# Block sums of streamed weights: made by transfers that add to their target, in place of GpSimd additions, in a two-block transformer kernel on one core

## The chip, the core and the metric

The kernel runs on one NeuronCore of one Trainium2 chip. The metric is the device time of one execution in microseconds (us). Five engines work side by side: TensorE (PE: matmuls, and PEld: its weight loads), VectorE (DVE), ScalarE (ACT), GpSimd (POOL) and SyncE (SP), which here only issues transfers. Data lies in SBUF (on chip, 128 partitions), in PSUM (eight banks of 128 x 512 words, where the matmuls accumulate) and in HBM, where the weights lie.

## The reference

Two transformer blocks are applied to one sequence of 512 tokens with width 1024, in 32-bit floats. What matters here is the last step of each block, a wide layer pair with 4096 hidden columns:

```
x = x + jnp.square(jax.nn.relu(h @ w_up[l])) @ w_down[l]
...
hid = jnp.square(jax.nn.relu(jnp.einsum('bsd,df->bsf', n2, w_up[l])))
mlp_out = jnp.einsum('bsf,fd->bsd', hid, w_down[l])
h = h + rms_norm_2(mlp_out, norm_mlp_post[l])
```

Before these steps come attention, a gated linear attention and cross attention in the first block, and a gated spatial layer and dilated attention in the second. The change does not touch them.

## The kernel before

**Precision.** Every 32-bit operand is split in two parts: a high part (made by ScalarE as a copy into a rounded type, `w_hi`, `a_hi`) and the rest (made by VectorE or GpSimd as a subtraction, `w_lo`, `a_lo`). Each product is three matmuls: high by high, low by high, high by low (lines 1236 to 1238).

**Weights.** They come as tiles of 128 x 1024 words (512 KB). SP issues their transfers in a fixed order, each behind a wait on `lo_w`, the count of the tiles that VectorE has split. Ordinary tiles land in two buffers `w_raw`; split tiles lie in eight slots of `w_hi` and `w_lo`. A tile is split when a slot is free, so VectorE's subtraction at line 1944 is what makes a `w_raw` buffer free for the next transfer.

**The wide layers.** The 4096 hidden columns are done in eight chunks of 512, in the order up(0), up(1), down(0), up(2), down(1), ... up(7), down(6), down(7). An `up` takes four tiles and gives `sq`, the squared hidden values (four PSUM banks, 96 matmuls). The first six `down` of each block are done with seven products of blocks instead of eight (a scheme of Strassen and Winograd): `block_sums` makes four sums s1 to s4 of blocks of `sq` on GpSimd, and the step `tsum` makes four sums t1 to t4 of the four weight tiles b11, b12, b21, b22. A product is 12 matmuls into two PSUM banks, (4, 5) for even products and (6, 7) for odd ones, and VectorE adds each bank to its target (line 2042, called draining the bank below). So product n+2 can start only when VectorE has drained the banks of product n. With the `up` this is 180 matmuls in a round of one `up` and one `down`; there are 12 rounds with seven products in the program.

**Order around the change.** Every engine walks through the same list of steps. In `up`, at its first step, ScalarE and VectorE split units 0 to 3 of the coming `down`, at its third step units 4 and 5, at its last step unit 6 (`tile_done` tells that a slot is free). During the products they split the four tiles of the next `up`, called raw 1 to raw 4 below, one after each of the products 0 to 3 (in half of the rounds inside the loop, after products 2 to 5). At a product, VectorE first drains the two banks and then splits what belongs to this step. The middle rounds are a hardware loop of two turns with two rounds each.

Of the kernel before, what the change touches and what calls it, by code (L numbers as in the profile page):

```python
# [31 lines left out]
ALU = mybir.AluOpType  # L32
# [84 lines left out]
UNITS = ("b11", "b21", "t2", "t1", "t3", "b22", "t4")  # L117
INTO = ("q1", (0, 0), "q6", "q5", "q7", (0, 1), (1, 0))
# [11 lines left out]
class Step:  # L130

    def __init__(self, kind, banks, fill, *, n=0, h=0, p=None, out=None, major=None, src=None, dst=None, rows=KC,
# [20 lines left out]
        self.nmax = nmax  # L154
        self.splits_lo = splits if splits_lo is None else splits_lo

class Schedule:
# [139 lines left out]
    def bank_steps(self, out, major, src, rows=KC, banks=4, halves=1, ready=None, blk=0, mid=None, dst=None, p=None,  # L298
# [77 lines left out]
    def products(self, dst, first=False):  # L376
# [68 lines left out]
def make_schedule():  # L445
# [103 lines left out]
    def run_mlp(dst, after_last, last):  # L549
# [172 lines left out]
    s.add("tsum", held=[s.n_down, 0], ready=all_out())  # L722
# [90 lines left out]
    s.add("tsum", held=[s.n_down, 0], ready=[])  # L813
# [45 lines left out]
def two_blocks(nc, a, out):  # L859

    s = make_schedule()
    with ExitStack() as ctx:
# [129 lines left out]
        t2 = place("t2", "mid", [WORDS], skip=28 * KB)  # L992
        t1 = place("t1", "more", [WORDS])
        t4 = place("t4", "more", [WORDS], skip=4 * KB)
        w_down = nc.alloc_sbuf_tensor_at("w_down", [P, 4, WORDS], F32, offset=base + region["const"] + phase)
        top_, low_ = slice(0, 2 * P), slice(2 * P, T)
        parts = (sq[:, 0:2, top_], sq[:, 2:4, top_], s2[:], s1[:], s3[:], s4[:], sq[:, 2:4, low_])
        part_sums = (0, 0, 3, 1, 2, 4, 0)
# [42 lines left out]
        down_in = [sem(f"down_in{n}") for n in range(4)]  # L1041
        sum_w = sem("sum_w")
# [44 lines left out]
        def landed(kind, raw):  # L1087
# [5 lines left out]
            if kind in ("t1", "t2", "t4"):  # L1093
                return {"t1": t1, "t2": t2, "t4": t4}[kind][:]
# [44 lines left out]
        def block_sums(eng, st, turn):  # L1139
# [3 lines left out]
            eng.tensor_tensor(s1[:], sq[:, 0:2, low_], sq[:, 2:4, low_], ALU.add).then_inc(sum_a, 1)  # L1143
            eng.wait_ge(sum_a, at(st.sum_a, turn, 1))
            eng.tensor_tensor(s3[:], sq[:, 0:2, top_], sq[:, 0:2, low_], ALU.subtract).then_inc(sum_a, 1)
            eng.tensor_tensor(s2[:], s1[:], sq[:, 0:2, top_], ALU.subtract).then_inc(sum_a, 1)
            eng.wait_ge(sum_a, at(st.sum_a, turn, 3))
            eng.tensor_tensor(s4[:], sq[:, 2:4, top_], s2[:], ALU.subtract).then_inc(sum_a, 1)

        def part_lo(eng, st, j, turn):  # L1150

            eng.wait_ge(hi_a, at(st.held, turn, j + 1))
            eng.tensor_tensor(a_lo[:, j], parts[j], a_hi[:, j], ALU.subtract).then_inc(lo_a, 1)

# [29 lines left out]
        def _(sp):  # L1184
# [7 lines left out]
            def load(kind, slot, tile, free, turn):  # L1192
                wait(sp, lo_w, at(free, turn))
                t = at(tile, turn)
                src = a["weights"][t] if isinstance(t, int) else a["weights"][bass.ds(t, 1)].rearrange("o p w -> p (o w)")
                if kind == "raw":
                    sp.dma_start(w_raw[:, slot, :], src).then_inc(raw_in[slot], 16)
                else:
                    sp.dma_start(w_down[:, slot, :], src).then_inc(down_in[slot], 16)
# [413 lines left out]
        def _(act):  # L1613
# [8 lines left out]
            def split(st, turn):  # L1622
                for n, slot, kind, raw, load, free in st.splits:
# [7 lines left out]
                    else:  # L1631
                        act.wait_ge(sum_w, at([4 * load[0], 4 * load[1]], turn, ("t1", "t2", "t3", "t4").index(kind) + 1))
# [298 lines left out]
        def _(dve):  # L1931
# [14 lines left out]
            def fold(st):  # L1946
# [5 lines left out]
                then(dve.tensor_tensor(q["q6"], q["q6"], q["q1"], ALU.add))  # L1952
                dve.tensor_tensor(x12, x12, q["q6"], ALU.add)
                then(dve.tensor_tensor(q["q7"], q["q7"], q["q6"], ALU.add))
                then(dve.tensor_tensor(x21, x21, q["q7"], ALU.add))
                if st.dst == "y":
                    dve.tensor_tensor(x22, q["q7"], q["q5"], ALU.add)
                else:
                    then(dve.tensor_tensor(q["q7"], q["q7"], q["q5"], ALU.add))
                    dve.tensor_tensor(x22, x22, q["q7"], ALU.add)  # L1960
# [649 lines left out]
```

## Time and profile before

| | |
|---|---|
| time, median of 3 runs (lowest to highest) | 1569.46 us (1569.41 to 1570.41) |
| span of the profiled execution | 1569.9 us |
| TensorE busy | 1553.6 us, 99% |
| VectorE busy | 989.6 us, 63% |
| ScalarE busy | 663.7 us, 42% |
| GpSimd busy | 483.5 us, 31% |
| moved by transfers | 164.34 MB, 105 GB/s over the span |
| granted TensorE clock in the windows read | 1.00 |

The profile names no other time for the profiled execution than its span. A row of a timeline gives the start, the duration, the engine, the line, the operation with target and sources, and in brackets how long the engine had been idle and on whom it waited. Where a row says x2, two operations were merged and the duration is that of both. The first wide layers lie at about 431 to 748 us, the second at about 1215 to 1561 us.

### The profile page before, as it was taken

The numbers are of one execution on the slowest core, as the hardware profiler recorded it, in microseconds if no ns is written. First come the engines' busy times: TensorE is split into PE (matmuls) and PEld (weight loads), VectorE is DVE, ScalarE is ACT, GpSimd is POOL, SyncE is SP. The second block draws the span as 40 slices with busy tenths as digits, with TensorE's granted clock in tenths as the row PEclk, the third lists the DMA queues.
The fourth block names the chain that finished last, engine by engine and source line by source line (L and its number), as shares of the span: only waits on it lengthen the run. The fifth ranks groups of instructions, "written<-read, shape, count | busy, mean of one in ns | idle before, by whom it ended". The sixth has DMA issues, their size and how long they took to land.

```text
span 1569.9 us, 21076 instructions
## 1 busy us (share of the span) xinstructions
PE 1553.6 (99%) x7772; PEld 1307.9 (83%) x7772; DVE 989.6 (63%) x1187; ACT 663.7 (42%) x1091; POOL 483.5 (31%) x283
## 2 busy tenths in 40 slices
PE   9999999999999999999999999999999999999998
PEld 7788888888888888888888898988888988888886
DVE  5453876335487777776664746347356677777766
ACT  5352565244354443443533334543334454434432
POOL 2442000000037776762310000020013047777732
PEclk9999999999999999999999999999999999999999
DMA  6422135321412232214232232343334322213133
GB/s 247 135 81 81 41 99 185 94 81 53 135 54 108 108 108 107 107 54 154 85 101 85 67 94 68 95 141 118 110 122 156 135 108 98 85 50 134 68 116 121
DMA packets 44997, 164.34 MB, mean 105 GB/s; under 512 B 5584, under 2 KB 5800, under 8 KB 44272
## 3 DMA queue, kind: packets, MB, share of 16 engines
q1 hardware_dynamic: 40608, 144.82, 28.4%
q0 software_dynamic: 4304, 18.36, 3.4%
q8 instruction: 56, 0.92, 0.2%
q14 instruction: 29, 0.24, 0.0%
HBM read 158.88 MB, written 5.85 MB: 105 GB/s over the span
## 4 chain that ended last, share of the span: by engine, by line
PE 94%; DVE 4%; ACT 1%; DMA 1%; issue 1%; POOL 0%; DVEq 0%; ACTq 0%; SPq 0%; POOLq 0%
PE banks L1236 29%; PE banks L1238 29%; PE banks L1237 29%; PE banks L1535 1%; PE banks L1414 1%; DVE nmax L2228 1%; DVE w_lo L1944 1%; DMA w_raw<-in_weights 1%; PE banks L1380 1%; PE banks L1353 0%; PE banks L1597 0%; DVE banks L2227 0%; PE banks L1573 0%; PE banks L1565 0%; PE banks L1524 0%
## 5 line engine op out<-in xcount | busy, mean ns | idle before, releaser
L1236 PE MATMUL banks<-act_hi,w_hi 128*128 128x512 f32 (+1 forms) x1088 | 413.3, 380 | 3.1 <-DVE act_lo L2110 3.1
L1944 DVE TENSOR_TENSOR w_lo<-w_raw,w_hi 128x1024 fp32r<-128x1024 f32 x216 | 280.4, 1304 | 208.4 <-ACT w_hi L1633 204.4
L1238 PE MATMUL banks<-act_hi,w_lo 128*128 128x512 f32 (+1 forms) x1088 | 409.9, 377 | 0.0
L1237 PE MATMUL banks<-act_lo,w_hi 128*128 128x512 f32 (+1 forms) x1088 | 409.9, 377 | 0.0
L1633 ACT ACTIVATE w_hi<-w_raw 128x1024 fp32r<-128x1024 f32 x216 | 227.1, 1060 | 259.2 <-DMA w_raw<-in_weights 205.3
L1236 PEld LDWEIGHTS banks<-act_hi,w_hi 128*128 128x128 f32 x1088 | 204.8, 188 | 41.0 <-issue 2.5
L1238 PEld LDWEIGHTS banks<-act_hi,w_lo 128*128 128x128 f32 x1088 | 204.7, 188 | 37.9
L1237 PEld LDWEIGHTS banks<-act_lo,w_hi 128*128 128x128 f32 x1088 | 204.8, 188 | 36.4
L1236 PE MATMUL banks<-w_hi,a_hi 128*128 128x512 f32 x400 | 155.8, 390 | 0.0
L1237 PE MATMUL banks<-w_lo,a_hi 128*128 128x512 f32 x400 | 155.6, 389 | 0.0
L1238 PE MATMUL banks<-w_hi,a_lo 128*128 128x512 f32 x400 | 155.6, 389 | 0.0
L1236 PE MATMUL banks<-w_hi,act_hi 128*128 128x512 f32 x352 | 139.6, 397 | 0.0
L1238 PE MATMUL banks<-w_hi,act_lo 128*128 128x512 f32 x352 | 137.7, 391 | 0.0
L1237 PE MATMUL banks<-w_lo,act_hi 128*128 128x512 f32 x352 | 137.6, 391 | 0.0
L1944 DVE TENSOR_TENSOR w_lo<-t,w_hi 128x1024 fp32r<-128x1024 f32 x36 | 87.3, 2450 | 40.2 <-ACT w_hi L1633 40.2
L2390 POOL TENSOR_TENSOR t<-w_down 128x1024 f32<-128x1024 f32 x12 | 39.6, 3298 | 171.2 <-DVE act_lo L2110 171.2
L1944 DVE TENSOR_TENSOR w_lo<-w_down,w_hi 128x1024 fp32r<-128x1024 f32 x48 | 82.8, 1760 | 13.8 <-ACT w_hi L1633 13.7
L1236 PEld LDWEIGHTS banks<-w_hi,a_hi 128*128 128x128 f32 x400 | 75.1, 188 | 16.0 <-DVE sums_y L2042 0.3
L1238 PEld LDWEIGHTS banks<-w_hi,a_lo 128*128 128x128 f32 x400 | 75.1, 188 | 15.8
L1237 PEld LDWEIGHTS banks<-w_lo,a_hi 128*128 128x128 f32 x400 | 75.1, 188 | 15.5
L1236 PEld LDWEIGHTS banks<-w_hi,act_hi 128*128 128x128 f32 x352 | 73.9, 210 | 12.3 <-issue 1.3
L1238 PEld LDWEIGHTS banks<-w_hi,act_lo 128*128 128x128 f32 x352 | 73.9, 210 | 11.4
(369 smaller groups left out, 2405.9 us busy)
## 6 DMA issues: line engine op xcount, KB each, us to landing
w_raw<-in_weights SPq DMA_DIRECT2D x216, 512.0 KB, 3.6
w_down<-in_weights SPq DMA_DIRECT2D x48, 512.0 KB, 6.1
wide<-share_dram POOLq DMA_DIRECT2D x3, 1024.0 KB, 11.9
x_tok<-in_x SPq DMA_DIRECT2D x4, 512.0 KB, 5.1
w_first<-in_weights SPq DMA_DIRECT2D x4, 512.0 KB, 8.1
x_tok<-in_x POOLq DMA_DIRECT2D x4, 512.0 KB, 5.1
x_dram<-x_tok POOLq DMA_DIRECT2D x1, 2048.0 KB, 8.1
x_tok<-x_dram POOLq DMA_DIRECT2D x1, 2048.0 KB, 8.9
```

Source lines behind the costliest of these rows:

```text
L1236: pe.matmul(out_ap, lhs[0], rhs[0], start=start, stop=False)
L1237: pe.matmul(out_ap, lhs[0], rhs[1], start=False, stop=False)
L1238: return pe.matmul(out_ap, lhs[1], rhs[0], start=False, stop=stop)
L1380: mm = pe.transpose(psum[:, n, tt * P:tt * P + P], rows[:, tt, c * P:c * P + P], ident[:])
L1414: mm = pe.matmul(psum[:, b, n * P // 2:(n + 1) * P // 2], lev[st.n % 2][rows, pair, tt * P:tt * P + P], right[rows, pair, tt, :, 1, :], st ...
L1535: mm = pe.matmul(psum[:, b, tt % 2 * M:tt % 2 * M + M], qx[:, 2 * st.h + e, tt * P:tt * P + P], kx[:, 2 * st.h + e, :], start=(e == 0), st ...
L1633: act.activation(w_hi[:, slot, :], landed(kind, raw), ACT.Copy).then_inc(hi_w, 1)
L1944: dve.tensor_tensor(w_lo[:, slot, :], landed(kind, raw), w_hi[:, slot, :], ALU.subtract).then_inc(lo_w, 1)
L2228: dve.tensor_reduce(nmax[:, h, i:i + 1], psum[:, b, c0:end], AX.X, ALU.max, negate=True).then_inc(smax, 1)
L2390: pool.tensor_tensor(t1[:], w_down[:, 1, :], w_down[:, 0, :], ALU.subtract).then_inc(sum_w, 1)
```

## The change

Four things are done.

1. The GpSimd additions of `tsum` are gone. SP now loads six tiles for a `down` instead of four: the four blocks, and tile 0 twice more, into the buffers t1 and t2. Then GpSimd's queue issues transfers that add to their target while they are written: t1 += tile 2, t2 += tile 2, `w_down` slot 1 += tile 3 (this is t3), and, when the first addition to t2 has landed, t2 += tile 3.
2. t4 has no buffer any more. It is made in t2, by one more adding transfer (t2 += tile 1) in a new step `tlast` between the third and the last step of `up`. It waits on `lo_w` until VectorE has split t2. The split of t4 is moved from the last step of `up` to product 0.
3. Since transfers can only add, signs are turned: s1, s2 and s4, the drains of the quarter (0, 1) and the `fold` subtract where they added. The units have another order.
4. The loop over the middle rounds is written out. With this the slots go round without a reset, and raw 1 to raw 4 are split after products 0 to 3 in every round.

```diff
-UNITS = ("b11", "b21", "t2", "t1", "t3", "b22", "t4")
-INTO = ("q1", (0, 0), "q6", "q5", "q7", (0, 1), (1, 0))
+UNITS = ("b11", "b21", "t1", "t3", "b22", "t2", "t4")
+INTO = ("q1", (0, 0), "q5", "q7", (0, 1), "q6", (1, 0))
...
-        for j in range(4):
-            self.load("down", j, 4 * g + (0, 2, 1, 3)[j], free)
+        for j in range(6):
+            self.load("down", j, 4 * g + (0, 2, 1, 3, 0, 0)[j], free)
...
-                self.add("tsum", held=self.cell(self.coming[0].load, "down"))
+                self.add("tsum", held=self.cell(self.coming[0].load, "down"), tile=self.cell(4 * (g + 1), "tile"))
+            if pairs and i == 3 and seven(g + 1):
+                self.add("tlast", held=self.placed(self.coming[5])[0], tile=self.cell(4 * (g + 1), "tile"))
...
-                at_step = {0: self.coming[0:4], 2: self.coming[4:6], 3: self.coming[6:7]}.get(i, [])
+                at_step = {0: self.coming[0:4], 2: self.coming[4:6]}.get(i, [])
                 when = [("tile", self.count("tile_done", 0), (2 if i == 3 else 0) + j) for j in range(2)]
+                if i == 3:
+                    self.last_free = [when[0]]
...
-            splits = []
+            splits = [self.split_of(self.mine[6], self.last_free)] if j == 0 else []
...
-        s.begin_loop((CHUNKS - 4) // 2)
-        for _ in range(2):
+        for _ in range(CHUNKS - 4):
             up()
             down()
-        s.end_loop()
...
-                    first = [4 * c for c in st.held]
                     landed_at = [16 * c for c in st.held]
-                    pool.wait_ge(down_in[0], at(landed_at, turn, 16))
+                    tile_of = lambda n: weights_tile(st.tile, turn, n)
+                    pool.wait_ge(down_in[4], at(landed_at, turn, 16))
+                    pool.dma_start(t1[:], tile_of(2), accum_op=ALU.add).then_inc(added["t1"], 16)
+                    pool.wait_ge(down_in[5], at(landed_at, turn, 16))
+                    pool.dma_start(t2[:], tile_of(2), accum_op=ALU.add).then_inc(added["t2"], 16)
                     pool.wait_ge(down_in[1], at(landed_at, turn, 16))
-                    pool.tensor_tensor(t1[:], w_down[:, 1, :], w_down[:, 0, :], ALU.subtract).then_inc(sum_w, 1)
-                    pool.wait_ge(down_in[3], at(landed_at, turn, 16))
-                    pool.wait_ge(sum_w, at(first, turn, 1))
-                    pool.tensor_tensor(t2[:], w_down[:, 3, :], t1[:], ALU.subtract).then_inc(sum_w, 1)
-                    pool.tensor_tensor(w_down[:, 1, :], w_down[:, 3, :], w_down[:, 1, :], ALU.subtract).then_inc(sum_w, 1)
-                    pool.wait_ge(down_in[2], at(landed_at, turn, 16))
-                    pool.wait_ge(sum_w, at(first, turn, 2))
-                    pool.tensor_tensor(t4[:], w_down[:, 2, :], t2[:], ALU.subtract).then_inc(sum_w, 1)
+                    pool.dma_start(w_down[:, 1, :], tile_of(3), accum_op=ALU.add).then_inc(added["t3"], 16)
+                    pool.wait_ge(added["t2"], at([32 * c for c in st.held], turn, 16))
+                    pool.dma_start(t2[:], tile_of(3), accum_op=ALU.add).then_inc(added["t2"], 16)
+                elif k == "tlast":
+                    pool.wait_ge(lo_w, at(st.held, turn, 1))
+                    pool.dma_start(t2[:], weights_tile(st.tile, turn, 1), accum_op=ALU.add).then_inc(added["t4"], 16)
```

Where the change moves instructions. First VectorE, from the third step of `up` to product 1, in the second round of the first block. `sq` are the squares of the hidden values, `w_lo` the splits of weight tiles, and rows that read `banks` are the drains. Before:

```order
L1944 TENSOR_TENSOR w_lo_53<-w_down_151,w_hi_52 128x1024 [waits hi_w,tile_done] x2
L1993 TENSOR_TENSOR sq_141<-sq_141 128x512 [waits bank_free2]
L1993 TENSOR_TENSOR sq_141<-sq_141 128x512 [waits bank_free3]
L1944 TENSOR_TENSOR w_lo_53<-t4_150,w_hi_52 128x1024 [waits hi_w,tile_done]
L2042 TENSOR_TENSOR sums_x_152<-banks,sums_x_152 128x512 [waits bank_done4]
L2042 TENSOR_TENSOR sums_x_152<-banks,sums_x_152 128x512 [waits bank_done5]
L1944 TENSOR_TENSOR w_lo_53<-w_raw_50,w_hi_52 128x1024 [waits hi_w,bank_done3]
L2042 TENSOR_TENSOR x_tok_49<-banks,x_tok_49 128x512 [waits bank_done6]
```

And in the changed kernel, at the same place:

```order
L1952 TENSOR_TENSOR w_lo_53<-w_down_150,w_hi_52 128x1024 [waits hi_w,tile_done]
L1952 TENSOR_TENSOR w_lo_53<-t2_149,w_hi_52 128x1024 [waits hi_w,tile_done]
L2001 TENSOR_TENSOR sq_141<-sq_141 128x512 [waits bank_free2]
L2001 TENSOR_TENSOR sq_141<-sq_141 128x512 [waits bank_free3]
L2055 TENSOR_TENSOR sums_x_151<-banks,sums_x_151 128x512 [waits bank_done4]
L2055 TENSOR_TENSOR sums_x_151<-banks,sums_x_151 128x512 [waits bank_done5]
L1952 TENSOR_TENSOR w_lo_53<-t2_149,w_hi_52 128x1024 [waits hi_w,tile_done]
L1952 TENSOR_TENSOR w_lo_53<-w_raw_50,w_hi_52 128x1024 [waits hi_w,bank_done3]
L2055 TENSOR_TENSOR x_tok_49<-banks,x_tok_49 128x512 [waits bank_done6]
```

The split of t4 stood ahead of the drains of product 0 and now stands behind them, directly ahead of the split of raw 1; the drains of product 1 come after both.

Then GpSimd, from the end of the products of one round to the block sums of the next. `s1` to `s3` are sums of blocks of `sq`. Before:

```order
L1153 TENSOR_TENSOR a_lo_147<-sq_141,a_hi_146 128x512 [waits hi_a]
L2390 TENSOR_TENSOR t1_149<-w_down_151 128x1024 [waits down_in1,down_in0]
L2393 TENSOR_TENSOR t2_148<-w_down_151,t1_149 128x1024 [waits sum_w,down_in3]
L2394 TENSOR_TENSOR w_down_151<-w_down_151 128x1024
L2397 TENSOR_TENSOR t4_150<-w_down_151,t2_148 128x1024 [waits sum_w,down_in2]
L1143 TENSOR_TENSOR s1_142<-sq_141 128x512 [waits lo_a,sq_made]
L1145 TENSOR_TENSOR s3_144<-sq_141 128x512 [waits sum_a]
L1146 TENSOR_TENSOR s2_143<-s1_142,sq_141 128x512
```

In the changed kernel:

```order
L1155 TENSOR_TENSOR a_lo_147<-sq_141,a_hi_146 128x512 [waits hi_a]
L2399 DMA t1_148<-in_weights 128x1024 [waits down_in4]
L2401 DMA t2_149<-in_weights 128x1024 [waits down_in5]
L2403 DMA w_down_150<-in_weights 128x1024 [waits down_in1]
L2405 DMA t2_149<-in_weights 128x1024 [waits added_t2]
L2408 DMA t2_149<-in_weights 128x1024 [waits lo_w]
L1145 TENSOR_TENSOR s1_142<-sq_141 128x512 [waits lo_a,sq_made]
L1147 TENSOR_TENSOR s3_144<-sq_141 128x512 [waits sum_a]
L1148 TENSOR_TENSOR s2_143<-s1_142,sq_141 128x512
```

Four additions became five transfers, and the fifth, which makes t4, hangs on VectorE's split of t2. The block sums behind them are where they were.

## Rows read from the trace of the kernel before

**Rows 1.** The page: busy times of the engines, and the chain of work by engine.

```profile
PE 1553.6 (99%) x7772; PEld 1307.9 (83%) x7772; DVE 989.6 (63%) x1187; ACT 663.7 (42%) x1091; POOL 483.5 (31%) x283
...
PE 94%; DVE 4%; ACT 1%; DMA 1%; issue 1%; POOL 0%; DVEq 0%; ACTq 0%; SPq 0%; POOLq 0%
```

**Rows 2.** Windows: stretch, its length, busy time of PE, PEld, DVE, ACT, POOL, clock.

```profile
520.00:560.00 40.00, 40.00 (x178) 33.14 (x177) 30.01 (x30) 16.64 (x22) 29.63 (x15) 1.00 0.29 105
```

**Rows 3.** Timeline of PE: the first matmul of certain products.

```profile
533.13 0.39 PE L1236 MATMUL banks<-w_hi,a_hi 128*128 128x512 f32 x1
...
557.61 0.39 PE L1236 MATMUL banks<-w_hi,a_hi 128*128 128x512 f32 x1
...
565.77 0.39 PE L1236 MATMUL banks<-w_hi,a_hi 128*128 128x512 f32 x1
...
573.94 0.40 PE L1236 MATMUL banks<-w_hi,a_hi 128*128 128x512 f32 x1
...
655.58 0.50 PE L1236 MATMUL banks<-w_hi,a_hi 128*128 128x512 f32 x1
```

**Rows 4.** Timeline of VectorE: drains (L2042) and splits (L1944) in three rounds.

```profile
531.71 1.28 DVE L2042 TENSOR_TENSOR sums_x<-banks,sums_x 128x512 f32<-128x512 f32 x2
...
537.66 4.81 DVE L1944 TENSOR_TENSOR w_lo<-w_down,w_hi 128x1024 fp32r<-128x1024 f32 x2 [0.92 <-ACT w_hi L1633]
...
552.64 2.35 DVE L1944 TENSOR_TENSOR w_lo<-w_down,w_hi 128x1024 fp32r<-128x1024 f32 x2
...
559.39 2.28 DVE L1944 TENSOR_TENSOR w_lo<-t,w_hi 128x1024 fp32r<-128x1024 f32 x1 [0.26 <-ACT w_hi L1633]
561.60 1.27 DVE L2042 TENSOR_TENSOR sums_x<-banks,sums_x 128x512 f32<-128x512 f32 x2
562.80 1.21 DVE L1944 TENSOR_TENSOR w_lo<-w_raw,w_hi 128x1024 fp32r<-128x1024 f32 x1
563.93 1.28 DVE L2042 TENSOR_TENSOR x_tok<-banks,x_tok 128x512 f32<-128x512 f32 x2
565.12 1.21 DVE L1944 TENSOR_TENSOR w_lo<-w_raw,w_hi 128x1024 fp32r<-128x1024 f32 x1
...
568.96 1.23 DVE L1944 TENSOR_TENSOR w_lo<-w_raw,w_hi 128x1024 fp32r<-128x1024 f32 x1 [1.43 <-ACT w_hi L1633]
570.11 1.28 DVE L2042 TENSOR_TENSOR sums_x<-banks,sums_x 128x512 f32<-128x512 f32 x2
571.84 1.23 DVE L1944 TENSOR_TENSOR w_lo<-w_raw,w_hi 128x1024 fp32r<-128x1024 f32 x1 [0.45 <-ACT w_hi L1633]
572.98 1.28 DVE L2042 TENSOR_TENSOR sums_x<-banks,sums_x 128x512 f32<-128x512 f32 x2
...
654.84 1.28 DVE L2042 TENSOR_TENSOR sums_x<-banks,sums_x 128x512 f32<-128x512 f32 x2
```

**Rows 5.** The page: costliest groups, the first addition of weight tiles.

```profile
L2390 POOL TENSOR_TENSOR t<-w_down 128x1024 f32<-128x1024 f32 x12 | 39.6, 3298 | 171.2 <-DVE act_lo L2110 171.2
```

**Rows 6.** Timeline of GpSimd: one addition of tiles, four block sums.

```profile
538.02 3.37 POOL L2390 TENSOR_TENSOR t<-w_down 128x1024 f32<-128x1024 f32 x1
...
559.30 1.29 POOL L1143 TENSOR_TENSOR s<-sq 128x512 f32<-128x512 f32 x1 [8.87 <-DVE sq L1993]
560.67 2.17 POOL L1145 TENSOR_TENSOR s<-sq 128x512 f32<-128x512 f32 x1
562.79 2.36 POOL L1146 TENSOR_TENSOR s<-s,sq 128x512 f32<-128x512 f32 x1
565.23 2.26 POOL L1148 TENSOR_TENSOR s<-sq,s 128x512 f32<-128x512 f32 x1
```

**Rows 7.** Timeline of ScalarE: the high part of unit 5.

```profile
552.37 1.06 ACT L1633 ACTIVATE w_hi<-w_down 128x1024 fp32r<-128x1024 f32 x1 [1.58 <-PE banks L1238]
```

**Rows 8.** Issues of transfers: two on GpSimd's queue; KB each, us to landing.

```profile
x_dram<-x_tok POOLq DMA_DIRECT2D x1, 2048.0 KB, 8.1
...
row<-in_norm_mlp_pre POOLq DMA_DIRECT2D x1, 512.0 KB, 4.5
```

More of the change, by code:

```diff
@@ L130, with __init__ @@
 class Step:
-    def __init__(self, kind, banks, fill, *, n=0, h=0, p=None, out=None, major=None, src=None, dst=None, rows=KC,
+    def __init__(self, kind, banks, fill, *, n=0, h=0, p=None, out=None, major=None, src=None, dst=None, rows=KC, tile=None,
                  half=0, first=False, splits=(), ready=None, bank=0, blk=0, mid=None,
@@ L154, in __init__ @@
         self.nmax = nmax
+        self.tile = tile
         self.splits_lo = splits if splits_lo is None else splits_lo
@@ L721, in make_schedule @@
     s.load_first()
-    s.add("tsum", held=[s.n_down, 0], ready=all_out())
+    s.add("tsum", held=[s.n_down, 0], tile=[4 * s.loaded[-1], 0])
     roped = [None]
@@ L812, in make_schedule @@
     s.add("row3", ready=ready())
-    s.add("tsum", held=[s.n_down, 0], ready=[])
+    s.add("tsum", held=[s.n_down, 0], tile=[4 * s.loaded[-1], 0])
     first = list(s.bank_steps("mix", "tok", "act", ready=merged_ready, blk=0))
@@ L1040, in two_blocks @@
         hi_made = sem("hi_made")
-        down_in = [sem(f"down_in{n}") for n in range(4)]
-        sum_w = sem("sum_w")
+        down_in = [sem(f"down_in{n}") for n in range(6)]
+        added = {name: sem(f"added_{name}") for name in ("t1", "t2", "t3", "t4")}
         tile_done = sem("tile_done")
@@ L1153, in part_lo, with weights_tile @@
             eng.tensor_tensor(a_lo[:, j], parts[j], a_hi[:, j], ALU.subtract).then_inc(lo_a, 1)
+        def weights_tile(tile, turn, n):
+            t = at(tile, turn, n)
+            return a["weights"][t] if isinstance(t, int) else a["weights"][bass.ds(t, 1)].rearrange("o p w -> p (o w)")
         def copies_of(st):
@@ L1193, in load @@
                 wait(sp, lo_w, at(free, turn))
-                t = at(tile, turn)
-                src = a["weights"][t] if isinstance(t, int) else a["weights"][bass.ds(t, 1)].rearrange("o p w -> p (o w)")
+                src = weights_tile(tile, turn, 0)
                 if kind == "raw":
@@ L1198, in load @@
                 else:
-                    sp.dma_start(w_down[:, slot, :], src).then_inc(down_in[slot], 16)
+                    into = w_down[:, slot, :] if slot < 4 else (t1, t2)[slot - 4][:]
+                    sp.dma_start(into, src).then_inc(down_in[slot], 16)
             n = 0
@@ L1631, in split @@
                     else:
-                        act.wait_ge(sum_w, at([4 * load[0], 4 * load[1]], turn, ("t1", "t2", "t3", "t4").index(kind) + 1))
+                        each_ = 32 if kind == "t2" else 16
+                        act.wait_ge(added[kind], at([each_ * load[0], each_ * load[1]], turn, each_))
                     act.activation(w_hi[:, slot, :], landed(kind, raw), ACT.Copy).then_inc(hi_w, 1)
@@ L1951, in fold @@
                 dve.tensor_tensor(x11, x11, q["q1"], ALU.add)
-                then(dve.tensor_tensor(q["q6"], q["q6"], q["q1"], ALU.add))
-                dve.tensor_tensor(x12, x12, q["q6"], ALU.add)
+                then(dve.tensor_tensor(q["q6"], q["q1"], q["q6"], ALU.subtract))
+                dve.tensor_tensor(x12, x12, q["q6"], ALU.subtract)
                 then(dve.tensor_tensor(q["q7"], q["q7"], q["q6"], ALU.add))
@@ L1956, in fold @@
                 if st.dst == "y":
[L1957 removed]
+                    dve.scalar_tensor_tensor(x22, q["q7"], -1.0, q["q5"], ALU.mult, ALU.subtract)
                 else:
                     then(dve.tensor_tensor(q["q7"], q["q7"], q["q5"], ALU.add))
[L1960 to L1961 removed]
+                    dve.tensor_tensor(x22, x22, q["q7"], ALU.subtract)
+                dve.tensor_tensor(x12, x12, q["q5"], ALU.subtract).then_inc(fold_made, 1)
                 dve.wait_ge(fold_made, "xy".index(st.dst) + 1)
@@ L2038, in handle @@
                             part = dst[:, 2 * rows + t, 512 * cols:512 * cols + 512]
-                        if st.first and (kept or st.dst == "y"):
+                        if INTO[st.n] == (0, 1):
+                            if st.first and st.dst == "y":
+                                dve.tensor_scalar(part, psum[:, b, :], -1.0, None, ALU.mult).then_inc(bank_free[b], 1)
+                            else:
+                                dve.tensor_tensor(part, part, psum[:, b, :], ALU.subtract).then_inc(bank_free[b], 1)
+                        elif st.first and (kept or st.dst == "y"):
                             dve.tensor_copy(part, psum[:, b, :]).then_inc(bank_free[b], 1)
```

18 lines of the change are left out of this document (7 added, 11 removed).

## The prediction

> **What bounds the kernel now.** I read the page first: TensorE is busy for 99% of the span and holds 94% of the chain of work [rows 1]. Then the windows of a round of the first wide layers: 40 us of 40 busy, at a granted clock of 1.00 [rows 2]. The timeline of TensorE gives the beat: from the first matmul of product 0 (557.61) to that of product 3 (565.77) are 36 matmuls in 8.16 us, 0.2267 us each, so a product lasts 2.72 us and a round of 180 matmuls 40.8 us. Product 6 begins at 533.13, 573.94 and 655.58, which is 40.81 us and two times 40.82 us apart, across the entry of the loop and its jump back [rows 3]. So nothing on GpSimd, and nothing of the loop, is on the path in these rounds: the most that a change there can win is the small bubble of about 0.1 us at 655.58, where a first matmul shows 0.50 in place of 0.39 us. What counts is whether the change makes TensorE wait.
>
> The place where that can happen is VectorE during the products. Product n+2 needs the banks of product n, so the drains of product 4 must have begun to finish when product 6 starts. In the round at 557.61 the pair of drains starts at 572.98 and its first half ends about 0.64 us later, at 573.62; product 6 starts at 573.94: 0.3 us to spare. In the round before, 531.71 + 0.64 = 532.35 against 533.13: 0.8 us. In the round of 655.58, 654.84 + 0.64 = 655.48: nothing, which is that bubble [rows 3, 4]. GpSimd and ScalarE have far more slack there.
>
> **The change part by part.**
>
> *The additions of tsum go.* Twelve times four operations of 2.4 to 3.4 us leave GpSimd [rows 5, 6]. While they ran, VectorE's splits took twice their time: two at 537.66 took 4.81 us, beside the addition at 538.02, while two at 552.64 took 2.35 us [rows 4, 6]. Those splits lie in `up`, where TensorE does not wait, so this is worth 0 to the 0.1 us bubble in a round. I take 0.
>
> *Seven more transfers of 512 KB a round* (two loads, five that add): 12 x 7 x 0.524 = 44 MB. The transfer engines are 29% busy in such a round at 105 GB/s [rows 2], so they have room; 0 for the traffic itself. Below nothing it can't be; above, it would delay the raw tiles, which I put under the rivals.
>
> *Signs, another order of units, the subtracting drains and fold:* as many operations of the same size as before; 0. *The loop written out:* 0, by the 40.82 us above; it also moves the splits of raw tiles in half of the rounds ahead to products 0 to 3, the pattern of the round at 557.61, which had 0.3 us to spare.
>
> *The split of t4 moves behind the drains of product 0.* Here the cost is. Take the round at 557.61. Before, the split of t4 starts at 559.39 and fills the time in which VectorE would wait for product 0 anyway; then come drains (561.60), raw 1 (562.80), drains (563.93) [rows 4]. After, the squares end at about 559.4, the drains of product 0 follow its end (557.61 + 2.72 = 560.33) and are through at about 561.2. Then VectorE has two splits in a row: t4 and raw 1. Alone these are two times 1.13 us (562.80 to 563.93), and would end at 563.5, even ahead of the 563.93 of before. But GpSimd is at its block sums. A split that meets a GpSimd operation waits for its end, and then GpSimd goes before the next split: the pair at 537.66 took 2.4 us each, and the split at 559.39 took 2.28 us because the sum s1 ran from 559.30 to 560.59 [rows 4, 6]. The sums s3 and s2 took 2.17 and 2.36 us for the same reason, against 1.29 for s1 [rows 6]. So after the change: s3 runs from 560.67 to 561.97; the split of t4 from 561.97 to 563.1; s2, which stood waiting, to 564.3; raw 1 to 565.4. That is 1.5 us later than before (563.93).
>
> Behind raw 1 wait: on VectorE the drains of product 1, which then have their first half at 566.0 against product 3 at 565.77 (0.3 us of TensorE); on SP the load of raw 3, which needs the buffer, and so in turn raw 3's split (568.96, which waited on ScalarE and that on the transfer), the drains of product 3 (570.11), raw 4 (571.84) and the drains of product 4 (572.98) [rows 3, 4]. Shifted by 1.5 us, these miss product 6 by 1.5 less the slack: 0.7, 1.2 and 1.5 us in the three rounds read, 1.1 us in the mean. The bubble at product 3 is part of it, not added, since it moves product 6 too.
>
> The Trainium skill ("SBUF — State Buffer", section "Who interferes with whom") says that a VectorE instruction with two SBUF inputs and a GpSimd instruction that reads SBUF exclude each other, and that the one which issues first holds the ports for its whole duration. The trace agrees, with 2.28 against 1.21 us [rows 4]; the same section has it that a drain, with one input in PSUM, doesn't contend, and with that the two splits standing side by side is the cost and their number is not.
>
> *Is t4 there in time?* t2's high part starts at 552.37, when TensorE frees the slot [rows 7], and its split ends at 554.99 [rows 4]. Only then can GpSimd issue t2 += tile 1. No row shows an adding transfer. The nearest is the copy of 512 KB on GpSimd's queue, 4.5 us; the 2048 KB one takes 8.1, so 512 KB more cost 1.2 us and the fixed part is 3.3 us [rows 8]. From below: 4.5 us, t4 lands at 559.5, its high part (1.06 us) is there at 560.6, ahead of 561.97. From above I take the data twice and t2 with it: rival 1. I take 4.5 us, the nearest row. t2 itself needs two adding transfers in a row, with t1's ahead: issued from 538.02 on, where the additions stood [rows 6], 538.0 + 4.5 + 1.2 + 4.5 = 548.2, ahead of 552.37.
>
> **Sum.** 12 rounds x 1.1 us = 13.6 us with unrounded shares. The span of the profiled execution is 1569.9 us, 0.4 above the median; 1583.5 for the span, **1583 us** for the median.
>
> **The rivals.**
>
> *Rival 1: t4 comes one turn late.* If the adding transfer lasts over 5.9 us from issue (561.97 - 1.06 - 554.99), s2 takes the ports at 561.97 and both splits come 1.2 to 1.3 us later: about 2.4 us a round, 29 us, 1599 us. With data time doubled to 2.4 us, a transfer takes 5.7 us and t2 lands at about 538.0 + 5.7 + 2 x 2.4 + 4.4 = 552.9 (t3 is ahead of it in the queue), 0.5 us late, so t4's high part ends near 562.3: over the edge. For it: that an addition has to read its target. Against it: no row.
>
> *Rival 2: adding transfers are much slower,* 8 us each. Then t2 lands near 555, t4's high part ends at 566.4 and raw 1's split near 568.7: 4.8 us late, 4.4 us a round, 1622 us.
>
> *Rival 3, the other side: no difference.* If GpSimd doesn't go between t4 and raw 1 (its s2 starts later, or VectorE keeps the ports), raw 1 ends at 561.97 + 2.26 = 564.2, 0.3 us late, within the slack of most rounds: 0 to 0.3 us a round, 1570 to 1573 us. It decides for this when the shift stays under the 0.3 us to spare. For it: at 562.80 the split went ahead of s2, whose row starts at 562.79. Against it: the pair at 537.66.
>
> *Rival 4: faster by over 3 us.* It would need TensorE waits that GpSimd's additions cause; the rounds show none but 0.1 us.
>
> **How the numbers follow.** Forecast (1578 to 1590) 0.38; rival 1 (1590 to 1605) 0.24; rival 2 0.06; rival 3 0.29; rival 4 0.03. A change of 0.2% (3.1 us) is about what a measurement of this kernel can tell from none. Slower: 0.38 + 0.24 + 0.06 less a little for a small version of the forecast, 0.66; the same 0.31; faster 0.03. The range leaves out rival 2, rival 4 and the end of rival 1: 1569 to 1602 us.
>
> **What the profile would show.** Right: the splits of t2's buffer in product 0 take over 2 us, raw 1's split starts about 1.5 us later against product 0 than now, first matmuls of products 3, 5 or 6 wait on VectorE drains about 1.1 us a round, 12 times, and the rest of the span is as it was. Rival 1: t4's high part waits on its transfer beyond 4.4 us after product 0's start. Rival 3: products 0 to 6 still last 19.04 us. The prediction is wrong if TensorE waits anywhere else, for instance for a weight tile whose transfer is late, or if VectorE's two splits stand free of GpSimd.

## The result, and the profile after

The changed kernel takes 1598.21 us (median of 4 runs, 1596.68 to 1603.0), the kernel before, on the same chip, 1569.93 us. The ratio is 1.018 (95% interval 1.0167 to 1.0192): it is slower by 28.3 us, where the forecast had 13.6 us. What the numbers fit is rival 1, with its 29 us. The profiled execution of the changed kernel took 1599.13 us with a span of 1597.3 us, at a granted clock of 1.00 of full speed.

The page of the changed kernel, with the lines that answer to [rows 1] and [rows 8]: busy times, GpSimd's DMA queue, the chain of work by engine, and the issues of transfers (KB each, us from issue to landing).

```profile
PE 1562.8 (98%) x7772; PEld 1306.9 (82%) x7772; DVE 937.1 (59%) x1187; ACT 662.4 (41%) x1091; POOL 379.0 (24%) x295
...
q0 software_dynamic: 12944, 49.82, 14.4%
...
PE 59%; DMA 13%; issue 11%; DVE 7%; POOL 5%; ACT 4%; SPq 0%; DVEq 0%; ACTq 0%; POOLq 0%
...
t<-in_weights POOLq DMA_DIRECT2D x48, 512.0 KB, 5.6
t<-in_weights SPq DMA_DIRECT2D x24, 512.0 KB, 8.7
```

GpSimd is relieved as announced, from 483.5 to 379.0 us busy, and VectorE too, from 989.6 to 937.1 us. But TensorE's share of the chain fell from 94% to 59%, and transfers, which had 1%, now hold 13%. GpSimd's additions had not been on the path (POOL held 0% of it), so nothing was taken off it, and a chain of transfers has come onto it.

Where TensorE stands idle, its timeline shows in the round whose product 0 starts at 561.41 (first matmuls of products 0, 3 and 5; the bracket is the idle time ahead and what ended it):

```profile
561.41 0.39 PE L1243 MATMUL banks<-w_hi,a_hi 128*128 128x512 f32 x1
...
571.00 0.47 PE L1243 MATMUL banks<-w_hi,a_hi 128*128 128x512 f32 x1 [1.27 <-DVE x_tok L2055]
...
577.33 0.47 PE L1243 MATMUL banks<-w_hi,a_hi 128*128 128x512 f32 x1 [0.63 <-DVE sums_x L2055]
```

Product 3 was due at 561.41 + 3 x 2.72 = 569.57 and starts 1.43 us late; product 5 loses 0.8 us more, and products 4 and 6 and the next `up` lose some 0.1 us each. Products 3 and 5 wait for drains on VectorE, as the prediction said, though for more. From the first matmul of product 0 to the first of the next `up` the seven products take 19.04 us in a round of the kernel before; here they take 21.60 (561.41 to 583.01). I read this length in all twelve rounds of each trace and added up what lies above 19.04. Before: 0.4 us in all. Changed: 1.36 and 1.83 us in the first round of the two blocks and 2.1 to 2.7 us in the other ten, 27.7 us together. That is the whole difference of the spans (1597.3 - 1569.9 = 27.4).

The timeline of VectorE for that round, with the split of t2 ahead of it; L1952 are splits, L2055 drains:

```profile
557.43 1.22 DVE L1952 TENSOR_TENSOR w_lo<-t,w_hi 128x1024 fp32r<-128x1024 f32 x1
...
564.33 0.69 DVE L2055 TENSOR_TENSOR sums_x<-banks,sums_x 128x512 f32<-128x512 f32 x1 [0.67 <-PE banks L1245]
565.69 2.33 DVE L1952 TENSOR_TENSOR w_lo<-t,w_hi 128x1024 fp32r<-128x1024 f32 x1 [0.67 <-ACT w_hi L1641]
567.95 2.30 DVE L1952 TENSOR_TENSOR w_lo<-w_raw,w_hi 128x1024 fp32r<-128x1024 f32 x1
570.17 1.28 DVE L2055 TENSOR_TENSOR x_tok<-banks,x_tok 128x512 f32<-128x512 f32 x2
```

The timeline of GpSimd: the transfer that makes t4 (L2408), and the block sums s1, s3, s2, s4.

```profile
559.02 0.88 POOL L2408 DMA_DIRECT2D t<-in_weights  x1 [7.60 <-DVE w_lo L1952]
563.02 1.29 POOL L1145 TENSOR_TENSOR s<-sq 128x512 f32<-128x512 f32 x1 [3.12 <-DVE sq L2001]
564.38 1.30 POOL L1147 TENSOR_TENSOR s<-sq 128x512 f32<-128x512 f32 x1
565.64 1.29 POOL L1148 TENSOR_TENSOR s<-s,sq 128x512 f32<-128x512 f32 x1
567.02 2.15 POOL L1150 TENSOR_TENSOR s<-s,sq 128x512 f32<-128x512 f32 x1
```

And ScalarE's high part of t4, which the split waits for:

```profile
564.53 1.06 ACT L1641 ACTIVATE w_hi<-t 128x1024 fp32r<-128x1024 f32 x1 [2.32 <-DMA t<-in_weights]
```

Read them together. VectorE is free of the drains of product 0 at 565.02 and waits 0.67 us for t4's high part, which ends at 565.59. Its split is there at 565.69; s2 has started at 565.64. By 0.05 us s2 has the ports, the split lasts 2.33 in place of 1.2 us, s4 gets its turn between the two splits, and raw 1 lasts 2.30. The drains of product 1 begin 570.17 - 561.41 = 8.76 us after product 0, where they began 6.32 us after it [rows 3, 4]: 2.44 us late. In the first round of all (product 0 at 475.79) the trace of the same kernel shows the other outcome. VectorE:

```profile
480.00 1.22 DVE L1952 TENSOR_TENSOR w_lo<-t,w_hi 128x1024 fp32r<-128x1024 f32 x1 [0.59 <-ACT w_hi L1641]
481.14 2.32 DVE L1952 TENSOR_TENSOR w_lo<-w_raw,w_hi 128x1024 fp32r<-128x1024 f32 x1
483.39 1.27 DVE L2055 TENSOR_TENSOR x_tok<-banks,x_tok 128x512 f32<-128x512 f32 x2
```

GpSimd:

```profile
480.03 2.36 POOL L1148 TENSOR_TENSOR s<-s,sq 128x512 f32<-128x512 f32 x1
```

Here the split came 0.03 us ahead of s2 and took its turn; s2 waited, and only raw 1 was slowed. This is the small step of the forecast, and the round lost 1.36 us.

The first round of the second block went the same way. In the other ten s2 starts 4.2 us after product 0 and t4's split comes behind it, by 0.05 to 0.22 us in four of them and by 0.3 to 2.2 us in the other six. In nine of the ten raw 1's split starts at the same moment, 6.5 us after product 0: once t4 has missed its turn, how far it missed it hardly counts. ScalarE in the round that missed it by most (product 0 at 604.77), the high part of t2 and then that of t4:

```profile
601.12 1.06 ACT L1641 ACTIVATE w_hi<-t 128x1024 fp32r<-128x1024 f32 x1 [0.21 <-DMA t<-in_weights]
...
610.00 1.06 ACT L1641 ACTIVATE w_hi<-t 128x1024 fp32r<-128x1024 f32 x1 [4.42 <-DMA t<-in_weights]
```

Here t2 too had waited for its transfer: its high part starts 3.65 us ahead of product 0, where it starts 5.24 us ahead in the round of 561.41 (556.17).

### The profile page after: what moved, and what is told of

Same layout as the page of the kernel before. It is cut to its first block, busy times and chain, and to the rows that moved or that the text cites. A ratio compares the mean times of both kernels' runs of the same rounds, so it can differ in the third digit from the quotient of the medians.

```text
span 1597.3 us, 20356 instructions
## 1 busy us (share of the span) xinstructions
PE 1562.8 (98%) x7772; PEld 1306.9 (82%) x7772; DVE 937.1 (59%) x1187; ACT 662.4 (41%) x1091; POOL 379.0 (24%) x295
## 4 chain that ended last, share of the span: by engine, by line
PE 59%; DMA 13%; issue 11%; DVE 7%; POOL 5%; ACT 4%; SPq 0%; DVEq 0%; ACTq 0%; POOLq 0%
PE banks L1243 18%; PE banks L1244 17%; PE banks L1245 17%; DMA t<-in_weights 10%; POOL a_lo L1155 4%; DVE w_lo L1952 4%; DMA w_raw<-in_weights 3%; ACT w_hi L1641 2%; PE banks L1542 1%; PE banks L1421 1%; DVE nmax L2241 1%; POOL t L2405 1%; PE banks L1604 0%; DVE banks L2240 0%; PE banks L1360 0%
## 5 line engine op out<-in xcount | busy, mean ns | idle before, releaser
L1952 DVE TENSOR_TENSOR w_lo<-w_raw,w_hi 128x1024 fp32r<-128x1024 f32 x216 | 286.4, 1331 | 210.6 <-ACT w_hi L1641 208.3
L1952 DVE TENSOR_TENSOR w_lo<-w_down,w_hi 128x1024 fp32r<-128x1024 f32 x48 | 62.6, 1323 | 54.2 <-ACT w_hi L1641 54.2
L1952 DVE TENSOR_TENSOR w_lo<-t,w_hi 128x1024 fp32r<-128x1024 f32 x36 | 50.5, 1403 | 62.8 <-ACT w_hi L1641 62.8
L1244 PEld LDWEIGHTS banks<-w_lo,act_hi 128*128 128x128 f32 x352 | 74.0, 210 | 10.7
## 6 DMA issues: line engine op xcount, KB each, us to landing
w_down<-in_weights POOLq DMA_DIRECT2D x12, 512.0 KB, 10.1
```

The costliest lines, as they stand in the source:

```text
L1244: pe.matmul(out_ap, lhs[0], rhs[1], start=False, stop=False)
L1952: dve.tensor_tensor(w_lo[:, slot, :], landed(kind, raw), w_hi[:, slot, :], ALU.subtract).then_inc(lo_w, 1)
```

## The experiments

All medians are of runs beside the kernel before on the same chip; its median was 1571.26 us for the first four, 1570.45 for the next four and 1571.73 for the last two. The column on the right is the time of the seven products above 19.04 us, summed over the twelve rounds of the profiled execution as above.

| Kernel | Median us | Ratio (95%) | Products, us |
|---|---|---|---|
| before | 1569.93 | 1 | 0.4 |
| changed | 1598.21 | 1.018 (1.0167-1.0192) | 27.7 |
| 1 before, loop written out | 1571.14 | 1.0003 (0.9993-1.0012) | 0.6 |
| 2 before, split of t4 moved | 1581.35 | 1.007 (1.0053-1.0087) | 9.6 |
| 3 changed, all block sums held | 1605.38 | 1.0226 (1.0208-1.0244) | 32.6 |
| 4 changed, t4 by a plain copy | 1585.23 | 1.0091 (1.0074-1.0107) | 13.7 |
| 5 before, split moved, sums held | 1576.12 | 1.0042 (1.0028-1.0055) | 5.3 |
| 6 changed, t4 added by GpSimd | 1571.94 | 1.0011 (1.0002-1.002) | 0.0 |
| 7 changed, t4's transfer early | 1585.23 | 1.009 (1.0075-1.0106) | 14.8 |
| 8 before, additions cut short | 1570.62 | 1.0005 (0.9996-1.0014) | 0.0 |
| 9 changed, only s2 held | 1579.69 | 1.0054 (1.0037-1.0071) | 9.0 |
| 10 changed, early and s2 held | 1573.6 | 1.0013 (1.0003-1.0022) | 1.0 |

**1. The loop written out.**

```diff
-        s.begin_loop((CHUNKS - 4) // 2)
-        for _ in range(2):
+        for _ in range(CHUNKS - 4):
             up()
             down()
-        s.end_loop()
```

> The kernel before, with the middle rounds written out and nothing else changed. Theory (late t4 and the two splits in a row cost TensorE 2.36 us a round, and nothing else does): within 0.2% of the kernel before, 1567 to 1573 us, since product 6 keeps its 40.8 us beat. Rival (the written-out rounds, whose raw splits all follow products 0 to 3, carry part of the loss): 1574 to 1584 us.

Measured: 1571.14 us, no difference. By itself the loop is no part of it.

**2. The split of t4 moved, nothing else.**

```diff
-                at_step = {0: self.coming[0:4], 2: self.coming[4:6], 3: self.coming[6:7]}.get(i, [])
+                at_step = {0: self.coming[0:4], 2: self.coming[4:6]}.get(i, [])
...
+                if i == 3:
+                    self.last_free = [when[0]]
...
-            splits = []
+            splits = [self.split_of(self.mine[6], self.last_free)] if j == 0 else []
```

> The kernel before (GpSimd additions, loop kept), with only the split of t4 moved to product 0, behind its drains. t4 is ready there long before. Theory (two splits in a row share the ports with the block sums; a t4 that is in time costs the smaller step): 0.7 to 1.4 us in each round whose raw 1 follows product 0, less where it follows product 2 (4 of 12 rounds): 1576 to 1586 us. Rival A (the whole loss is in the move, whatever the time of t4): 1594 to 1602 us. Rival B (the whole loss is transfers, their traffic or their lateness): 1567 to 1573 us.

Measured: 1581.35 us, the small step. It is not spread evenly: four of the twelve rounds, which were every second one inside the loop, lose nothing. VectorE in one of them (product 0 at 601.26):

```profile
604.79 1.82 DVE L1946 TENSOR_TENSOR w_lo<-t,w_hi 128x1024 fp32r<-128x1024 f32 x1
606.53 1.28 DVE L2044 TENSOR_TENSOR x_tok<-banks,x_tok 128x512 f32<-128x512 f32 x2
```

Behind the split of t4 the drains of product 1 come at once: in these rounds no raw tile is split behind product 0. The pair is needed for the loss, and the written-out loop puts it into all twelve rounds. So the loop costs nothing alone, but with the moved split it makes four more rounds pay: 13.7 us in experiment 4 against 9.6 here.

**3. All block sums held until raw 1 is split.**

```diff
-        sums = self.add("sums", counts={"sum_a": 4}, sq=squared, held=self.count("lo_a", 0)).sum_a
+        sums = self.add("sums", counts={"sum_a": 4}, sq=squared, held=self.count("lo_a", 0), of=self.placed(self.coming[0])[0]).sum_a
...
+                    pool.wait_ge(lo_w, at(st.of, turn, 1))
                     block_sums(pool, st, turn)
```

> The changed kernel, with GpSimd's block sums held until VectorE has split raw 1, so that no GpSimd operation lies beside the two splits. Theory (the ports cost 2 x 1.1 us in these splits): t4's split runs about 4.3 to 5.5 us after product 0 starts, raw 1's to 6.6, the drains of product 1 are in time, and 0 to 0.4 us a round remain: 1569 to 1575 us. Rival (the lateness of t4 and the traffic of the transfers by themselves): it stays at 1592 to 1600 us.

Measured: 1605.38 us, slower still; this expectation fell. The splits themselves do what was expected. VectorE in the round whose product 0 starts at 562.24:

```profile
568.68 1.23 DVE L1952 TENSOR_TENSOR w_lo<-t,w_hi 128x1024 fp32r<-128x1024 f32 x1 [2.83 <-ACT w_hi L1641]
569.82 1.22 DVE L1952 TENSOR_TENSOR w_lo<-w_raw,w_hi 128x1024 fp32r<-128x1024 f32 x1
```

Alone they last 1.2 us. But VectorE had waited 2.83 us for t4: GpSimd's queue carries the transfers too, behind the sums and a_lo. From its timeline:

```profile
571.12 1.27 POOL L1145 TENSOR_TENSOR s<-sq 128x512 f32<-128x512 f32 x1 [8.30 <-DVE w_lo L1952]
...
588.94 0.87 POOL L2399 DMA_DIRECT2D t<-in_weights  x1
```

s1 starts 8.9 us after product 0 in place of 1.6, the first adding transfer is issued 26.7 us after it in place of 24.1, t1, t2 and t4 follow late, and late t4 holds the next sums. I had costed GpSimd's delay at nothing, for an engine 24% busy, and had not asked what else stands in its queue.

Late transfers are not all of it. In the round of 650.93 t4's split starts 4.45 us after product 0 and the drains of product 1 after 6.72, and still the round loses 2.1 us, at products 5 and 6. VectorE at raw 3 and raw 4 there:

```profile
662.84 2.23 DVE L1952 TENSOR_TENSOR w_lo<-w_raw,w_hi 128x1024 fp32r<-128x1024 f32 x1 [1.44 <-ACT w_hi L1641]
...
666.18 2.36 DVE L1952 TENSOR_TENSOR w_lo<-w_raw,w_hi 128x1024 fp32r<-128x1024 f32 x1
```

The held sums and the `a_lo` behind them run beside these two splits instead (GpSimd is at s4 from 662.69 and at `a_lo` from 663.94): the hold has moved the clash as well as the transfers.

**4. t4's transfer a plain copy** (t4 is then tile 1 alone: this kernel leaves out the sum with t2).

```diff
-                    pool.dma_start(t2[:], weights_tile(st.tile, turn, 1), accum_op=ALU.add).then_inc(added["t4"], 16)
+                    pool.dma_start(t2[:], weights_tile(st.tile, turn, 1)).then_inc(added["t4"], 16)
```

> The changed kernel, with the last transfer of a round, t2 += tile 1, made a plain copy of tile 1. So t4 is wrong: the addition to t2 is left out. Theory (t4's high part misses its turn before the sum s2 by under 0.1 us, because the adding transfer lasts 5.4 us where a copy takes some 4.5): t4's split goes ahead of s2 and about 1.2 us a round are saved, 1580 to 1588 us. Rival (it is not the moment of t4 but the two splits and the sums in any order, or the traffic): 1594 to 1600 us.

Measured: 1585.23 us, 13.7 us over twelve rounds or 1.14 each; the large step has become the small one. This is the cleanest pair of the study: one argument of one transfer. The transfers in a window about t4's in the changed kernel (558 to 570), queue and issue:

```profile
q0 software_dynamic: 144, 0.52, 25.7%
...
t<-in_weights POOLq DMA_DIRECT2D x1, 512.0 KB, 5.4
```

and in this kernel (556 to 568):

```profile
q0 software_dynamic: 144, 0.52, 13.3%
...
t<-in_weights POOLq DMA_DIRECT2D x1, 512.0 KB, 4.0
```

The same 144 packets and 0.52 MB occupy the transfer engines 1.93 times as long when they add, and land 1.4 us later (over the twelve rounds the transfer of t4 takes 5.1 to 5.8 us against 3.7 to 4.1). With that, t4's split (562.82) goes ahead of s2 (563.53), and only raw 1 pays. VectorE:

```profile
562.82 1.83 DVE L1952 TENSOR_TENSOR w_lo<-t,w_hi 128x1024 fp32r<-128x1024 f32 x1
564.57 2.31 DVE L1952 TENSOR_TENSOR w_lo<-w_raw,w_hi 128x1024 fp32r<-128x1024 f32 x1
566.80 1.28 DVE L2055 TENSOR_TENSOR x_tok<-banks,x_tok 128x512 f32<-128x512 f32 x2
```

The drains of product 1 begin 566.80 - 559.29 = 7.51 us after product 0.

**5. The kernel before, split moved and sums held** (the edits of 2 and 3 together).

> The kernel before with the split of t4 behind the drains of product 0, and with GpSimd's block sums held back until raw tile 1 is split. Nothing is transferred that adds, so no transfer can be late when GpSimd's work starts later. Theory (the two splits lose time only because the block sums share SBUF's ports with them): both splits last 1.2 us, the drains of product 1 come where they came before, 1569 to 1575 us. Rival (a split more in front of the drains of product 1 costs by itself, or GpSimd's later start costs elsewhere): 1579 us or more, as without the hold (1581.35).

Measured: 1576.12 us, 1.1 above the expected range. It is 5.7 us above the kernel before on its chip, where experiment 2 was 10.1 above on its own. Ten of the twelve rounds lose nothing at all; four of these have no pair of splits (the loop is kept, as in experiment 2), so it is six of the eight rounds with the pair that the hold has freed. VectorE in the round of 557.49:

```profile
561.02 1.22 DVE L1946 TENSOR_TENSOR w_lo<-t,w_hi 128x1024 fp32r<-128x1024 f32 x1
562.15 1.22 DVE L1946 TENSOR_TENSOR w_lo<-w_raw,w_hi 128x1024 fp32r<-128x1024 f32 x1
563.29 1.28 DVE L2044 TENSOR_TENSOR x_tok<-banks,x_tok 128x512 f32<-128x512 f32 x2
...
636.04 3.43 DVE L1946 TENSOR_TENSOR w_lo<-t,w_hi 128x1024 fp32r<-128x1024 f32 x1
```

The same move, the same pair, and the drains begin after 5.80 us, even ahead of the 6.32 of before. So in these six rounds a split more behind product 0 is free; the ports shared with the block sums are the cost. Two rounds lose 2.6 us each and the layer behind the first block's last round 1.1. Ahead of one of the two stands the last row above, a split of 3.43 us, beside a GpSimd addition at its own place in the queue, now later than before:

```profile
635.00 3.39 POOL L2399 TENSOR_TENSOR t<-w_down,t 128x1024 f32<-128x1024 f32 x1
```

The other of the two shows the same two rows, a split of 3.43 us beside an addition of 3.39. That this collision is the whole of their loss was not tried by itself.

**6. The changed kernel with t4 alone added by GpSimd,** into a buffer of its own, and split where it was.

```diff
-                at_step = {0: self.coming[0:4], 2: self.coming[4:6]}.get(i, [])
+                at_step = {0: self.coming[0:4], 2: self.coming[4:6], 3: self.coming[6:7]}.get(i, [])
...
+        t4 = place("t4", "mid", [WORDS], skip=28 * KB)
...
-                    pool.dma_start(t2[:], weights_tile(st.tile, turn, 1), accum_op=ALU.add).then_inc(added["t4"], 16)
+                    pool.wait_ge(down_in[2], at([16 * c for c in st.held], turn, 16))
+                    pool.wait_ge(added["t2"], at([32 * c for c in st.held], turn, 32))
...
+                    pool.tensor_tensor(t4[:], t2[:], w_down[:, 2, :], ALU.add).then_inc(added["t4"], 1)
```

> The changed kernel, but t4 alone is made by a GpSimd addition (t2 plus tile 1, into a buffer of its own) and split where the kernel before splits it, in the fourth step of `up`. The adding transfers for t1, t2 and t3, the six loads, the new order of units, the turned signs and the written-out loop stay. Theory (all of the loss hangs on t4's late transfer and late split): 1569 to 1573 us. Rival (the other transfers, or the order of the units, cost something of their own): 1576 us or more.

Measured: 1571.94 us, within 0.2% of before, and no round above 19.07 us. Two loads and four of the five adding transfers a round, the order of units, the signs and the written-out loop are all in it. None of them costs anything that shows.

**7. t4's addition started when t2 has landed,** in a buffer of its own that holds a copy of tile 1 (one copy more a round).

```diff
+                    pool.dma_start(t4[:], tile_of(1)).then_inc(t4_in, 16)
...
-                    pool.wait_ge(lo_w, at(st.held, turn, 1))
-                    pool.dma_start(t2[:], weights_tile(st.tile, turn, 1), accum_op=ALU.add).then_inc(added["t4"], 16)
+                    pool.wait_ge(t4_in, at([16 * c for c in st.held], turn, 16))
+                    pool.wait_ge(added["t2"], at([32 * c for c in st.held], turn, 32))
+                    pool.dma_start(t4[:], t2[:], accum_op=ALU.add).then_inc(added["t4"], 16)
```

> The changed kernel, but t4 has a buffer of its own: a copy of tile 1 goes into it early, and t2 is added to it by a transfer that starts when t2 has landed instead of when t2 has been split, some 3 us sooner; the split stays behind the drains of product 0. Theory (the large step comes from t4's high part being ready about 0.1 us too late for its turn): the step is the small one, as with a plain copy, 1580 to 1588 us. Rival (the transfer's lateness is not it, or one transfer more delays t2 as much as it gains): 1594 us or more.

Measured: 1585.23 us, the small step again, now with the full computation. It is the arrival of t4 that decides the turn, not that it is added.

**8. The additions cut to 16 columns** in the kernel before (this kernel leaves out the sums of tiles).

```diff
-                return {"t1": t1, "t2": t2, "t4": t4}[kind][:]
+                return w_down[:, {"t1": 0, "t2": 3, "t4": 2}[kind], :]
...
-                    pool.tensor_tensor(t1[:], w_down[:, 1, :], w_down[:, 0, :], ALU.subtract).then_inc(sum_w, 1)
+                    pool.tensor_tensor(t1[:, :16], w_down[:, 1, :16], w_down[:, 0, :16], ALU.subtract).then_inc(sum_w, 1)
```

> The kernel before with GpSimd's four additions of weight tiles cut to 16 columns each; the units t1, t2 and t4 are then read from tiles 0, 3 and 1 as loaded, and no sum of tiles is computed for them. It is the most that taking these additions off GpSimd can bring. Theory (they lie beside other work): 1567 to 1570.5 us, at most 2 us below the kernel before. Rival (the additions hold up the splits in `up` and so TensorE): 1565 us or less.

Measured: 1570.62 us, no difference. Taking the additions off GpSimd could bring nothing clear of the interval (0.9996 to 1.0014), whatever takes their place.

**9. Only s2 held until raw 1 is split.**

```diff
+            if st.kind == "sums":
+                eng.wait_ge(lo_w, at(st.of, turn, 1))
             eng.tensor_tensor(s2[:], s1[:], sq[:, 0:2, top_], ALU.add).then_inc(sum_a, 1)
```

> The changed kernel with one wait more: GpSimd's third block sum, s2, stands back until raw tile 1 is split (s1 and s3 run as they did; the run that held all four sums moved GpSimd's later work, and with it the transfers, by 3 us a round). The transfer that makes t4 is as slow as in the changed kernel. Theory (a late t4 is dear only because s2 then takes the turn): t4's split starts at about 4.3 us after product 0's start and raw 1's ends at about 6.7 us, 0.3 to 0.5 us later than in the kernel before, 1572 to 1580 us. Rival (the held sums push GpSimd's later work and the transfers, as the hold of all four did): 1590 us or more.

Measured: 1579.69 us, just inside. Both splits are undisturbed; VectorE in the round of 556.80:

```profile
562.53 1.22 DVE L1954 TENSOR_TENSOR w_lo<-t,w_hi 128x1024 fp32r<-128x1024 f32 x1 [2.12 <-ACT w_hi L1643]
563.67 1.22 DVE L1954 TENSOR_TENSOR w_lo<-w_raw,w_hi 128x1024 fp32r<-128x1024 f32 x1
```

What is left goes with the lateness of t4: its split starts after 5.73 us here, and the round loses 1.6 us; in the round of 599.22 it starts after 4.41, and the loss is 0.25. The expectation had 4.3 and so 0.3 to 0.5 us a round; the rounds lost 0 to 2.2, in the mean 0.75. The hold is not what made t4 late, as its rival had it: the first adding transfer of a round is issued 19.2 to 19.5 us ahead of product 0 here and in the changed kernel alike (read in the rounds behind the first of each block). The delay comes in through t2. Its high part starts 5.24 us ahead of product 0 when it needn't wait for its transfer, 4.12 us ahead in the round of 556.80 and 3.42 us ahead in the one that loses 2.2; the changed kernel had such rounds too (3.65 in that of 604.77), but there they cost little more, since raw 1 stood behind s2's turn anyway.

**10. Both mends, of 7 and 9.**

> The changed kernel with both mends: t4 in a buffer of its own with the addition started once t2 has landed, and s2 held back until raw tile 1 is split. Theory: both splits of the pair last about 1.2 us and raw 1's ends where it ended before, 1569 to 1577 us, no better than the kernel before since TensorE is the bound there. Rival (the wait only moves the clash to later splits at the same price): 1581 us or more.

Measured: 1573.6 us, within 0.2% of before. VectorE in the round of 556.11:

```profile
559.63 1.84 DVE L1957 TENSOR_TENSOR w_lo<-t,w_hi 128x1024 fp32r<-128x1024 f32 x1
561.39 1.21 DVE L1957 TENSOR_TENSOR w_lo<-w_raw,w_hi 128x1024 fp32r<-128x1024 f32 x1
562.53 1.28 DVE L2060 TENSOR_TENSOR x_tok<-banks,x_tok 128x512 f32<-128x512 f32 x2
```

One split meets s3 and lasts 1.84; with s2 held, raw 1 is free of GpSimd, and the drains of product 1 begin after 6.42 us. All block sums of weights are made by transfers here, and next to nothing is lost (1.0 us of the products); nothing is won either. No version beat the kernel before: with TensorE at 99% there was nothing for it to win.

## Why the prediction was wrong

- **What bounds the kernel** was right: experiment 8 puts the gain from GpSimd's additions at nothing.
- **Traffic, signs, the order of units: 0** was right (experiment 6). **The loop: 0** was right alone (experiment 1), and the prediction said that it moves raw tiles to products 0 to 3; experiment 2 shows what that is worth together with the move.
- **The split of t4 behind product 0: 1.1 us a round** was right as a mechanism and as a size, for a t4 that is in time: 1.14 us in experiment 4. The drains of product 1 come 1.2 us late there, a little less than the 1.5 worked out. That the sizes agree so well is partly luck, since the loss falls elsewhere: in experiment 4 product 3 starts 0.2 us late and product 5 another 0.4 to 0.9 us, where the prediction had 0.3 at product 3 and the rest at product 6. That ports shared with the block sums are the cause, and not one split more, experiment 5 shows with the six rounds that have the pair and still last 19.04 us.
- **"Is t4 there in time?" is the step that failed.** It took 4.5 us, the nearest row of a copy, from the end of t2's split until t4's high part could start. Measured in the round of 561.41: 564.53 - 558.65 = 5.88 us. Of this, 0.37 us pass between the end of the split and the issue, which I had costed at nothing, and nearly all of the rest is the transfer, 5.4 us by its own row, with a copy at 4.0 in experiment 4. The edge that the prediction named for rival 1 was 5.9 us; by that this round would just have been in time. But s2 started 4.23 us after product 0, where the prediction had 4.36 (561.97 against 557.61), and t4's split came 0.05 us behind it. The other term of this step failed as well: t2 was to have landed at 548.2, 9.4 us ahead of product 0. Of the three additions issued together, the one to t1 landed after 5.4 to 6.0 us, that to t2 after 7.4 to 8.9, that to `w_down` after 9.3 to 10.8, against 4.5 for the first and 5.7 for the second in the sum; t2 itself landed 5.7 us ahead of product 0 in the round of 561.41 and 3.7 in that of 604.77. In five of the ten rounds t2's high part starts 0.2 to 1.6 us later than the 5.24 us ahead of product 0 at which TensorE frees its slot, and t4 moves with it. Rival 1 had t2 4.7 us ahead (552.9). Its price, 2.4 us a round, was right: 27.7 / 12 = 2.3.
- **The weighing of row and rule.** Experiment 4 now gives the row that was missing. The rule of the Trainium skill ("Collectives: The Full Stack", section "The bandwidth ceiling: the fold count and why AG ≠ RS ≠ AR"), which that section states for the adding step of a collective, agrees with its 1.93 times the engine time. I had given more chance to the nearest row, which was of another kind of operation. The rule named by "SBUF — State Buffer", section "Who interferes with whom", agrees too, with 1.22 us for a split alone in experiment 5 and 2.33 beside s2. What made the step so large is the order, which the prediction had read rightly: between two splits that stand ready, GpSimd's waiting operation goes first. With s2 held (experiment 9) a t4 as late as this cost 0.75 us a round in place of 2.3.

## What to carry to other kernels

Before work is taken off an engine, cut it to almost nothing in place and time that (experiment 8): if it brings nothing, a replacement can only lose. When an operation moves next to another on VectorE, look at what GpSimd does in those microseconds, and treat the arrival of its operand as a deadline against GpSimd's start: missing it cost 1.2 us a round here, whether by 0.05 us or by 1. And where a chain of transfers has to meet it, add up each of them as measured beside the others. And a wait put on a lightly used engine also holds the transfers in its queue.

## What the hardware showed that I had not expected

- A transfer of 512 KB that adds to its target in SBUF took 5.4 us from issue to landing, with nothing beside it, and a copy 4.0 us (5.1 to 5.8 and 3.7 to 4.1 over the rounds of the two kernels); the transfer engines were occupied 25.7% and 13.3% of 12 us by the two. An addition from SBUF to SBUF landed after 4.5 us (median of 12 in experiment 10, and the same in experiment 7).
- Three additions of 512 KB issued within 1.5 us of each other on GpSimd's queue, beside SyncE's loads, landed after 5.5, 7.4 and 9.3 us in the round of 561.41, and after 5.9, 8.9 and 10.8 in that of 604.77.
- Two VectorE splits in a row beside a queue of GpSimd sums took 2.33 and 2.30 us where each takes 1.22 alone (1.22 and 1.22 in experiment 5): the two engines took turns, operation by operation.
